# Attention scores and values from stacked high and low halves, with the two row halves of the values summed on VectorE

## The chip, the core and the metric

The kernel runs on one core of a Trainium2 chip. The metric is the device time in microseconds (us) from launch to the end; every time here is of that one core. The engines are TensorE (PE in the profile; its weight loads are PEld), VectorE (DVE), ScalarE (ACT), GpSimd (POOL), and SyncE (SP), which here only issues DMAs.

## The reference

One inference step of a decoder layer for 1024 prompt tokens and 8 sample tokens (T = 1032 rows of 1024 features). The input projection `z = rms_norm(x) @ w_in` gives three convolution inputs, queries (16 heads of 64), keys and values (4 key heads of 64) and two gates. The attention is causal within a window of 128:

```python
def attend(q, k, v, q_pos, k_pos, rel_bias, sinks):
    s = jnp.einsum('...qkgd,...skd->...kgqs', qg, k,
                   preferred_element_type=jnp.float32) * (HEAD_DIM ** -0.5)
...
    s = jnp.where(valid[..., None, None, :, :], s + bias, -jnp.inf)
    m = jnp.maximum(jnp.max(s, axis=-1, keepdims=True), sink)
    p = jnp.exp(s - m)
    p = p / (jnp.sum(p, axis=-1, keepdims=True) + jnp.exp(sink - m))
    o = jnp.einsum('...kgqs,...skd->...qkgd', p.astype(v.dtype), v)
```

The prompt is cut into 8 blocks of 128 queries; a block looks at its own 128 keys and the 128 before. Convolution and attention outputs are projected, gated, added, projected again, and followed by a mixture of 32 experts. All data are float32.

## The kernel before

**Products.** Almost every float32 product is made from two parts: x is rounded to a "high" part (type fp32r, a reduced float32 that TensorE takes) and the rest is the "low" part. The product is the sum of three fp32r matmuls, high*high, high*low and low*high, accumulated in PSUM. ScalarE writes the high part with a copy, VectorE subtracts it from the original to get the low part. Weights come in units of 1024 rows by 128 columns (`w_raw`, three slots), are split to `w_hi` and `w_lo` (`split_hi` L1127, `split_lo` L1433), and are used in three chunks of 344 tokens, 24 matmuls each, into the PSUM banks `DN[0..2]`.

**Stages.** (A) Ten weight units for queries and keys, into `q_sb` and `k_sb`; (V) two units for the values, nine chunks of 24 matmuls, into `v_sb`; (B) the prompt's attention, woven into the 24 units of the convolution inputs; (C) 32 units of output projections and gates; then the output projection with routing, and the experts.

**Stage B** is what the change is about. It runs 8 blocks (`step_b(j)`); block j makes three convolution units and the attention of query block j. A block has nine steps i = 0..8. In step i TensorE does, in this order of its program (L830 to L850):

- `scores(i)` for i < 8 (L796): two heads at once (one in partitions 0 to 63, the other in 64 to 127), each one plain float32 matmul of 64 rows: 128 queries by 256 keys, from `q_stage` and `k_stage`, into PSUM banks `SCB`. It waits for `max_ready` of step i-1;
- the 24 matmuls of convolution chunk i (L847 to L849), k = 0..7. Between them stand `values` (at k = 2 of steps 3, 5, 7 for steps 1, 3, 5, and at k = 5 of the next block's step 0 for step 7) and `turn_probs(i-1)` at k = 5 (L806, four transposes of the probabilities).

`values` (L825 to L827) makes, for each of two key heads and each of two key tiles, three matmuls of 256 columns: `v_hi`*`probsT_hi`, `v_hi`*`probsT_lo`, `v_lo`*`probsT_hi`. The stationary operand holds both key heads of a pair, 128 columns, so that half of the 128 result rows is of use; the other half is thrown away. Twelve matmuls for a full block, six in block 0, which has one key tile.

VectorE in step i, in order: maxima of the scores with the bias (L1543 to L1549, `max_ready`), in step 1 the low part of v (L1555), the inverse of the sums (L1512, L1513; waits for ScalarE's exponentials), the low part of the turned probabilities of step i-1 (L1563; waits for ScalarE's high part, and so for TensorE's transposes), in steps 6 and 7 the convolution itself (L1570 to L1576), `leave(i)`, which takes chunk i out of PSUM (L1524, L1527, L1532; waits for TensorE's chunk i), and in steps 0, 3, 6 one `split_lo` (L1433). ScalarE in step i: exponentials (L1183, L1184), high part of the turned probabilities of step i-1 (L1192), `store_o` (L1165; in step 6 and in the next block's step 1: the attention output from PSUM to `q_sb`), the scaling of the probabilities (L1199, `probs_normed`, for which `turn_probs` waits), and in steps 0, 3, 6 `split_hi`. GpSimd copies the next block's k and q to `k_stage` and `q_stage` (L551, L552) once the eight scores of a block are done.

Engines run their own programs in order and wait on semaphores. The order is written out by hand.

**Weight slots.** SyncE loads a unit into `w_raw[slot]` once the slot's `split_lo` is done (`lo_ready`); `w_lo` is a buffer of its own.

## Time and profile before

| | us |
|---|---|
| three runs | 1740.86, 1736.86, 1737.24 |
| median | 1737.24 |
| profiled execution: its own time | 1738.65 |
| profiled execution: span of the trace | 1737.1 |
| stage B in the trace: first scores to the first chunk of C | 187.8 to 585 |

The profile was taken on one execution; its own time is 1.4 us above the median, and 1.5 us of it lie outside the span of the trace. In rows of the timeline the first number is the start, the second the length; matmuls overlap their neighbours, so the price of one matmul is the distance between two starts and not its length. "x4" means that so many instructions are merged in one row; the plain float32 matmuls leave two records each. A pair in brackets at the end of a row gives the idle time of the engine before it and who ended it.

### The profile page before, as it was taken

Reading aid. Unit: us, or ns where it says so; the run is one execution under the profiler, and the core shown is the slowest. Engines: PE = TensorE matmul, PEld = TensorE weight load, DVE = VectorE, ACT = ScalarE, POOL = GpSimd, SP = SyncE. Lnnn points to the kernel's source line nnn. Section 1 sums busy time; section 2 is a strip of 40 time slices with the busy share of each in tenths; the row PEclk is TensorE's granted clock in tenths of the full one; section 3 lists DMA queues with packets and bytes.
Section 4 is the critical chain, followed back from the end, with each engine's and each line's share of the span. In section 5 each row is a group of like instructions: output and inputs, shape, how many; then the busy total and the mean of one; then the engine's idle time right before and its main releaser. Section 6 shows DMA issues by size and latency. Waiting matters only on the chain. (4 is left out here: it accounts for less than half of the span.)

```text
span 1737.1 us, 26183 instructions
## 1 busy us (share of the span) xinstructions
PE 1653.6 (95%) x9527; PEld 1474.4 (85%) x9527; DVE 1036.5 (60%) x1839; ACT 834.0 (48%) x1202; POOL 234.0 (13%) x197
## 2 busy tenths in 40 slices
PE   5999999999999999999999999699999999999991
PEld 4899899999999999999999888478888888877871
DVE  5322466656556432114222576788989899888883
ACT  5000355555555430113112211378788888877773
POOL 1100000000000100000000111322322323222310
PEclk9999999999999999999999999799999999999996
DMA  6242111111111301114113711799999999999956
GB/s 161 79 125 86 40 41 46 49 36 36 36 49 48 101 25 49 49 36 158 41 44 120 255 73 72 266 379 375 379 375 372 381 370 380 373 368 367 365 206 218
DMA packets 131856, 305.30 MB, mean 176 GB/s; under 512 B 30403, under 2 KB 92079, under 8 KB 106935
## 3 DMA queue, kind: packets, MB, share of 16 engines
q1 hardware_dynamic: 115415, 267.76, 42.2%
q0 software_dynamic: 16384, 36.76, 7.3%
q8 instruction: 38, 0.62, 0.1%
q14 instruction: 19, 0.16, 0.0%
HBM read 282.81 MB, written 40.41 MB: 186 GB/s over the span
## 5 line engine op out<-in xcount | busy, mean ns | idle before, releaser
L1847 DVE TENSOR_TENSOR e_lo<-e_raw,e_hi 128x2048 fp32r<-128x2048 f32 x192 | 434.5, 2287 | 58.6 <-ACT e_hi L1332 34.1
L1332 ACT ACTIVATE e_hi<-e_raw 128x2048 fp32r<-128x2048 f32 x192 | 366.1, 1921 | 64.6 <-PE bank L1033 30.2
L1031 PE MATMUL bank<-e_hi,xT_hi 128*128 128x512 f32 x512 | 206.8, 404 | 6.7 <-DVE xT_lo L1852 6.7
L1127 ACT ACTIVATE w_hi<-w_raw 128x1024 fp32r<-128x1024 f32 x68 | 71.6, 1053 | 284.4 <-PE bank L704 252.8
L702 PE MATMUL bank<-h_hi,w_hi 128*128 128x344 f32 x624 | 202.8, 325 | 1.1 <-DVE h_lo L1452 1.1
L1033 PE MATMUL bank<-e_hi,xT_lo 128*128 128x512 f32 x512 | 202.5, 395 | 0.0
L1032 PE MATMUL bank<-e_lo,xT_hi 128*128 128x512 f32 x512 | 201.9, 394 | 0.0
L703 PE MATMUL bank<-h_lo,w_hi 128*128 128x344 f32 x624 | 199.9, 320 | 0.0
L704 PE MATMUL bank<-h_hi,w_lo 128*128 128x344 f32 x624 | 199.8, 320 | 0.0
L847 PE MATMUL bank<-h_hi,w_hi 128*128 128x344 f32 x576 | 197.3, 342 | 2.0 <-DVE w_lo L1433 2.0
L848 PE MATMUL bank<-h_lo,w_hi 128*128 128x344 f32 x576 | 184.8, 321 | 0.0
L849 PE MATMUL bank<-h_hi,w_lo 128*128 128x344 f32 x576 | 184.4, 320 | 0.0
L1433 DVE TENSOR_TENSOR w_lo<-w_raw,w_hi 128x1024 fp32r<-128x1024 f32 x68 | 84.6, 1245 | 153.5 <-ACT w_hi L1127 152.4
L1183 ACT ACTIVATE probs<-probs,negm 128x256 f32<-128x256 f32 (+1 forms) x128 | 62.4, 488 | 140.1 <-DVE sinkd L1549 140.1
L847 PEld LDWEIGHTS bank<-h_hi,w_hi 128*128 128x128 f32 x576 | 108.8, 189 | 21.6 <-issue 9.9
L1031 PEld LDWEIGHTS bank<-e_hi,xT_hi 128*128 128x128 f32 x512 | 96.6, 189 | 32.1 <-issue 6.7
L702 PEld LDWEIGHTS bank<-h_hi,w_hi 128*128 128x128 f32 x624 | 117.9, 189 | 5.0 <-issue 3.5
L704 PEld LDWEIGHTS bank<-h_hi,w_lo 128*128 128x128 f32 x624 | 118.0, 189 | 0.0
L703 PEld LDWEIGHTS bank<-h_lo,w_hi 128*128 128x128 f32 x624 | 117.8, 189 | 0.0
L1033 PEld LDWEIGHTS bank<-e_hi,xT_lo 128*128 128x128 f32 x512 | 96.7, 189 | 23.1
L1032 PEld LDWEIGHTS bank<-e_lo,xT_hi 128*128 128x128 f32 x512 | 96.7, 189 | 20.5
L848 PEld LDWEIGHTS bank<-h_lo,w_hi 128*128 128x128 f32 x576 | 109.2, 190 | 0.0
(327 smaller groups left out, 3134.6 us busy)
## 6 DMA issues: line engine op xcount, KB each, us to landing
e_raw<-in_w_e_gate_dram SPq DMA_DIRECT2D x64, 1024.0 KB
e_raw<-in_w_e_up_dram SPq DMA_DIRECT2D x64, 1024.0 KB
e_raw<-in_w_e_down_dram SPq DMA_DIRECT2D x64, 1024.0 KB
w_raw<-in_w_in_dram SPq DMA_DIRECT2D x104, 256.0 KB, 3.1
a_spill<-y_sb POOLq DMA_DIRECT2D x8, 516.0 KB, 2.9
a_raw<-a_spill SPq DMA_DIRECT2D x2, 2064.0 KB, 9.6
x_tok<-in_x_prompt_dram SPq DMA_DIRECT2D x4, 1024.0 KB, 10.7
w_raw<-in_w_attn_out_dram SPq DMA_DIRECT2D x32, 128.0 KB, 2.9
```

Source lines behind the costliest of these rows:

```text
L702: pe.matmul(out, wh, xh, start=i == 0, stop=False)
L703: pe.matmul(out, wh, xl, start=False, stop=False)
L704: mm = pe.matmul(out, wl, xh, start=False, stop=i == len(pairs) - 1)
L847: pe.matmul(DN[c][:, 0:CH], w_hi[:, s, k, :], h_hi[:, k, cols], start=k == 0, stop=False)
L848: pe.matmul(DN[c][:, 0:CH], w_hi[:, s, k, :], h_lo[:, k, cols], start=False, stop=False)
L849: mm = pe.matmul(DN[c][:, 0:CH], w_lo[:, s, k, :], h_hi[:, k, cols], start=False, stop=k == KT - 1)
L1031: pe.matmul(out, xT_hi[:, par, kk, :], wh, start=kk == 0, stop=False)
L1032: pe.matmul(out, xT_hi[:, par, kk, :], wl, start=False, stop=False)
L1033: mm = pe.matmul(out, xT_lo[:, par, kk, :], wh, start=False, stop=kk == KT - 1)
L1332: A.activation(e_hi[:, slot % 4, :], e_raw[slot][:, :], ACT.Copy).then_inc(e_hi_done, 1)
L1433: V.tensor_tensor(w_lo[:, slot, :, :], w_raw[slot][:, :, :], w_hi[:, slot, :, :].bitcast(F32), ALU.subtract).then_inc(lo_ready, 1)
L1847: V.tensor_tensor(e_lo[slot][:, :], e_raw[slot][:, :], e_hi[:, slot % 4, :].bitcast(F32), ALU.subtract).then_inc(e_lo_done, 1)
```

## The change

- **Scores.** `q_a` holds, for the even head, the high part of q in partitions 0 to 63 and its low part in 64 to 127; `q_b` the same for the odd head with the halves the other way round. `kk_hi` holds the high part of k twice, in both halves; `kk_lo` the low part twice. One fp32r matmul over all 128 rows gives (q_hi + q_lo) * k_hi; a second (q_hi + q_lo) * k_lo. So four fp32r matmuls of 256 columns stand where two plain float32 ones of 64 rows stood.
- **Values.** `vv` holds for each key head its high and low columns side by side as one 128-column stationary operand. Two matmuls (with `probsT_hi`, with `probsT_lo`) take the place of three; one half of the result rows is from v_hi, the other from v_lo, and both are needed.
- **New work.** GpSimd makes the high parts in their own halves (four copies of 64 partitions per four steps, `stage`); ScalarE makes the two copies of k's high part in the other halves (`twin`); VectorE makes the low parts (`stage_low`, six subtractions of 64 partitions); ScalarE now copies the result half of the low part to `o_rest`, and VectorE adds it to the other half (`add_rest`), which takes over `o_stored`. Each of these is done twice per block, for heads 0 to 7 (t = 0) and 8 to 15 (t = 1).
- **Buffers.** To make room, `w_lo` now lies on top of `w_raw`, slot by slot. A slot is free for the next load only when TensorE has used it (`chunk_done`), and the slots of the units are renumbered.

```diff
-        q_stage = at("q_stage", R5, [KT, P])
-        k_stage = at("k_stage", R5 + 4096, [2, 2 * P])
+        q_a = at("q_a", R5, [KT, P], F32R)
+        q_b = at("q_b", RING + 24576, [KT, P], F32R)
+        kk_hi = at("kk_hi", RING + 28672, [KV, 2 * P], F32R)
+        kk_lo = at("kk_lo", RING + 32768, [KV, 2 * P], F32R)
...
-        w_lo = at("w_lo", RING + 24576, [3, KT, P], F32R)
+        w_lo = at("w_lo", RING, [3, KT, P], F32R)
...
+        twin_done, TWIN_FROM = sqrt_done, 3
+        stage_lo, STAGE_FROM = x_scaled, 9
+        rest_done, REST_FROM = h_hi_done, 16
...
                 if wait is not None:
-                    sp.wait_ge(lo_ready, wait)
+                    sp.wait_ge(chunk_done, wait)
...
+            def stage(b, t):
+
+                if not isinstance(b, int):
+                    pool.wait_ge(scores_ready, b * 8 + (4 * t - 4))
+                st = slice(4 * t, 4 * t + 4)
+                pool.tensor_copy(q_a[0:64, st, :], q_sb[0:64, st, bass.ds(b * P, P)])
+                pool.tensor_copy(q_b[64:128, st, :], q_sb[64:128, st, bass.ds(b * P, P)])
...
+                pool.tensor_copy(kk_hi[0:64, 2 * t, keys], k_sb[0:64, bass.ds(t, 1), old].rearrange("p a s -> p (a s)"))
+                pool.tensor_copy(kk_hi[64:128, 2 * t + 1, keys], k_sb[64:128, bass.ds(t, 1), old].rearrange("p a s -> p (a s)")).then_inc(staged, 1)
...
-                if st == 0:
-                    pe.wait_ge(staged, b * 2 + 2)
+                if st % 4 == 0:
+                    pe.wait_ge(staged, b * 2 + (t + 1))
+                    pe.wait_ge(twin_done, b * 2 + (TWIN_FROM + t + 1))
+                    pe.wait_ge(stage_lo, b * 2 + (STAGE_FROM + t + 1))
...
                 for h in range(2):
-                    mm = pe.matmul(SCB[h][:, place + off:place + 256], q_stage[64 * h:64 * h + 64, st, :],
-                                   k_stage[64 * h:64 * h + 64, t, off:256], start=True, stop=True)
+                    q2, out = (q_a, q_b)[h], SCB[h][:, place + off:place + 256]
+                    pe.matmul(out, q2[:, st, :], kk_hi[:, 2 * t + h, off:256], start=True, stop=False)
+                    mm = pe.matmul(out, q2[:, st, :], kk_lo[:, 2 * t + h, off:256], start=False, stop=True)
...
-                        vh, vl = v_hi[:, kt, P * t:P * t + P], v_lo[:, kt, P * t:P * t + P]
-                        ph, pl = probsT_hi[:, h, kt, :, :], probsT_lo[:, h, kt, :, :]
-                        pe.matmul(out, vh, ph, start=kt == kts[0], stop=False)
-                        pe.matmul(out, vh, pl, start=False, stop=False)
-                        mm = pe.matmul(out, vl, ph, start=False, stop=kt == 1)
+                        v2 = vv[:, kt, t, 2 * h:2 * h + 2, :].rearrange("p a d -> p (a d)")
+                        pe.matmul(out, v2, probsT_hi[:, h, kt, :, :], start=kt == kts[0], stop=False)
+                        mm = pe.matmul(out, v2, probsT_lo[:, h, kt, :, :], start=False, stop=kt == 1)
...
                 for h in range(2):
-                    rows = slice(64 * h, 64 * h + 64)
-                    ins = A.activation(q_sb[rows, 4 * t:4 * t + 4, bass.ds(b * P, P)], OB[h][rows, :].rearrange("p (k t) -> p k t", k=4), ACT.Copy)
-                ins.then_inc(o_stored, 1)
+                    ins = A.activation(o_rest[64 * h:64 * h + 64, :], OB[h][64 - 64 * h:128 - 64 * h, :], ACT.Copy)
+                ins.then_inc(rest_done, 1)
...
+                A.activation(kk_hi[64:128, 2 * t, keys], k_sb[0:64, t, old], ACT.Copy)
+                A.activation(kk_hi[0:64, 2 * t + 1, keys], k_sb[64:128, t, old], ACT.Copy).then_inc(twin_done, 1)
...
+            def stage_low(b, t, first=False):
+
+                dve.wait_ge(staged, b * 2 + (t + 1))
+                dve.wait_ge(twin_done, b * 2 + (TWIN_FROM + t + 1))
...
+                V.tensor_tensor(q_a[64:128, st, :], q_sb[0:64, st, now], q_a[0:64, st, :].bitcast(F32), ALU.subtract)
+                V.tensor_tensor(q_b[0:64, st, :], q_sb[64:128, st, now], q_b[64:128, st, :].bitcast(F32), ALU.subtract)
...
+                    for dst in (own, other):
+                        ins = V.tensor_tensor(kk_lo[dst, 2 * t + h, keys], k_sb[own, t, old], kk_hi[own, 2 * t + h, keys].bitcast(F32), ALU.subtract)
+                ins.then_inc(stage_lo, 1)
+
+            def add_rest(t, b):
+
+                dve.wait_ge(rest_done, b * 2 + (REST_FROM + t + 1))
+                for h in range(2):
+                    rows = slice(64 * h, 64 * h + 64)
+                    ins = V.tensor_tensor(q_sb[rows, 4 * t:4 * t + 4, bass.ds(b * P, P)], o_rest[rows, :].rearrange("p (k t) -> p k t", k=4),
+                                          OB[h][rows, :].rearrange("p (k t) -> p k t", k=4), ALU.add)
+                ins.then_inc(o_stored, 1)
...
                 for i in range(9):
+                    if i == 2 and not first:
+                        stage_low(j, 1)
+                    if i == 5 and not last:
+                        stage_low(j + 1, 0)
...
+                    if i == 1 and not first:
+                        add_rest(1, j - 1)
+                    if i == 6:
+                        add_rest(0, j)
...
+            stage_low(0, 0, True)
+            stage_low(0, 1, True)
```

ScalarE calls `twin(j, 1)` at the start of step 2 and `twin(j + 1, 0)` at the start of step 5, VectorE `stage_low` at the same two places. Before block 0 VectorE has `stage_low(0, 0)` and `stage_low(0, 1)` behind its last work of stage V.

The order on VectorE, from the low part of v in step 1 to the maxima of step 2. Before:

```order
L1555 TENSOR_TENSOR v_lo<-v_sb,v_hi 128x512
L1512 TENSOR_TENSOR rden<-den,esink 128x2
...
L1513 RECIPROCAL rden<-rden 128x2
L1563 TENSOR_TENSOR probsT_lo<-bank,probsT_hi 128x4x128
...
L1524 COPY u_sb<-bank 128x344
...
L1540 MEMSET carrier 128x1
```

and now:

```order
L1530 TENSOR_TENSOR rden<-den,esink 128x2
...
L1612 TENSOR_TENSOR probsT_lo<-bank,probsT_hi 128x4x128
...
L1553 TENSOR_TENSOR q_sb<-o_rest,bank 64x4x128
...
L1566 COPY u_sb<-bank 128x344
...
L1539 TENSOR_TENSOR q_a<-q_sb,q_a 64x512
...
L1540 TENSOR_TENSOR q_b<-q_sb,q_b 64x512
...
L1545 TENSOR_TENSOR kk_lo<-k_sb,kk_hi 64x256 x2
...
L1586 MEMSET carrier 128x1
```

Two additions (L1553 stands twice) now come before `leave(1)`, and six subtractions (L1545 stands twice, two each) between `leave(1)` and the maxima of step 2, which begin with the MEMSET. In front of the maxima of step 5 the same six stand, and in step 6 the two additions behind the low part of the probabilities.

The order on TensorE at a step's start, between the last matmul of one convolution chunk and the first of the next:

```order
L865 MATMUL bank<-h_hi,w_lo 128x344
L814 MATMUL bank<-kk_hi,q_a 128x256
L815 MATMUL bank<-kk_lo,q_a 128x256
L814 MATMUL bank<-kk_hi,q_b 128x256
L815 MATMUL bank<-kk_lo,q_b 128x256
L863 MATMUL bank<-h_hi,w_hi 128x344
```

Before, one row stood there, L796, with its two matmuls of 64 rows; nothing else of TensorE's order at this place moved.

## Rows read from the trace of the kernel before

**Rows 1.** The page's engines; a window of stage B (PE, PEld, DVE, ACT, POOL, clock)
```profile
PE 1653.6 (95%) x9527; PEld 1474.4 (85%) x9527; DVE 1036.5 (60%) x1839; ACT 834.0 (48%) x1202; POOL 234.0 (13%) x197
...
260.00:640.00 380.00, 380.00 (x2550) 348.65 (x2549) 209.58 (x680) 189.27 (x496) 23.22 (x25) 0.99 0.15 48
```

**Rows 2.** Timeline of PE, scores of steps 0, 1, 2 of a block, and the next block
```profile
333.64 0.70 PE L796 MATMUL bank<-k_stage,q_stage 64*128 64x256 f32 x4
339.69 0.70 PE L796 MATMUL bank<-k_stage,q_stage 64*128 64x256 f32 x4
344.72 0.70 PE L796 MATMUL bank<-k_stage,q_stage 64*128 64x256 f32 x4
...
383.59 0.70 PE L796 MATMUL bank<-k_stage,q_stage 64*128 64x256 f32 x4
```

**Rows 3.** Timeline of PE around one pair of scores
```profile
399.50 0.31 PE L849 MATMUL bank<-h_hi,w_lo 128*128 128x344 f32 x1
399.74 0.70 PE L796 MATMUL bank<-k_stage,q_stage 64*128 64x256 f32 x4
400.37 0.42 PE L847 MATMUL bank<-h_hi,w_hi 128*128 128x344 f32 x1
400.63 0.32 PE L848 MATMUL bank<-h_lo,w_hi 128*128 128x344 f32 x1
```

**Rows 4.** The same at the end of a `values`; then line L827 alone
```profile
402.59 0.28 PE L826 MATMUL bank<-probsT_lo,v_hi 128*128 128x256 f32 x1
402.71 0.28 PE L827 MATMUL bank<-probsT_hi,v_lo 128*128 128x256 f32 x1
...
L827 PE MATMUL bank<-probsT_hi,v_lo x120: 277/280/283, 206.8 to 584.7; 128*128 128x256 f32 x120
```

**Rows 5.** Timeline of DVE, steps 3 to 5 of a block
```profile
357.38 1.22 DVE L1433 TENSOR_TENSOR w_lo<-w_raw,w_hi 128x1024 fp32r<-128x1024 f32 x1 [0.51 <-ACT w_hi L1127]
358.53 0.48 DVE L1543 CUSTOM_DVE_ANT_0 probs<-bank,bias_sb,sink 128x256 f32<-128x256 f32 x1
...
362.17 0.50 DVE L1527 TENSOR_TENSOR u_sb<-u_sb,bank 128x344 f32<-128x344 f32 x1
362.60 0.48 DVE L1543 CUSTOM_DVE_ANT_0 probs<-bank,bias_sb,sink 128x256 f32<-128x256 f32 x1
```

**Rows 6.** Timeline of DVE, then of POOL, from step 6 to step 7 of a block
```profile
372.15 0.69 DVE L1563 TENSOR_TENSOR probsT_lo<-bank,probsT_hi 128x512 fp32r<-128x512 f32 x1 [0.56 <-ACT probsT_hi L1192]
...
375.35 0.99 DVE L1574 SCALAR_TENSOR_TENSOR y_sb<-histT,cols,y_sb 128x8 f32<-128x8 f32 x1
...
377.62 0.48 DVE L1543 CUSTOM_DVE_ANT_0 probs<-bank,bias_sb,sink 128x256 f32<-128x256 f32 x1
...
374.29 2.04 POOL L552 COPY q_stage<-q_sb 128x1024 f32 x1
```

**Rows 7.** Timeline of ACT: `store_o` in step 6, scaling of step 7, two blocks
```profile
330.69 0.90 ACT L1199 ACTIVATE probs<-probs,rden 128x256 f32<-128x256 f32 x2
372.01 1.18 ACT L1165 ACTIVATE q_sb<-bank 64x512 f32 x2
380.65 0.90 ACT L1199 ACTIVATE probs<-probs,rden 128x256 f32<-128x256 f32 x2
```

**Rows 8.** Timeline of DVE, steps 0 and 1 of a block
```profile
339.79 0.52 DVE L1524 COPY u_sb<-bank 128x344 f32<-128x344 f32 x1 [2.16 <-PE bank L849]
...
341.37 0.48 DVE L1543 CUSTOM_DVE_ANT_0 probs<-bank,bias_sb,sink 128x256 f32<-128x256 f32 x1
```

**Rows 9.** Groups by line and form: 512 elements in blocks 1 to 7, 256 in block 0
```profile
L1555 DVE TENSOR_TENSOR v_lo<-v_sb,v_hi 128x512 fp32r<-128x512 f32 x7 | 4.8, 693 | 0.5
...
L1563 DVE TENSOR_TENSOR probsT_lo<-bank,probsT_hi 128x256 fp32r<-128x256 f32 x8 | 3.4, 422 | 4.3 <-ACT probsT_hi L1192 4.3
```

**Rows 10.** Timeline of PE at the start of stage B, then a window (clock 0.50)
```profile
187.83 0.49 PE L796 MATMUL bank<-k_stage,q_stage 64*128 64x128 f32 x4
190.36 0.42 PE L847 MATMUL bank<-h_hi,w_hi 128*128 128x344 f32 x1 [2.04 <-DVE w_lo L1433]
...
192.00:194.00 2.00, 2.00 (x8) 2.00 (x8) 0.19 (x2) 1.73 (x6) 0.00 (x0) 0.50 0.79 236
```

**Rows 11.** Timeline of PE, start of stage V
```profile
160.69 0.58 PE L780 MATMUL bank<-w_hi,h_hi 128*128 128x256 f32 x1 [3.13 <-DVE w_lo L1433]
```

More of the change, by code:

```diff
@@ L559, in _ @@
             pool.wait_ge(bias_loaded, 16)
-            stage(0, True)
+            for t in range(2):
+                stage(0, t)
             flat = lambda x: x.rearrange("b s g d -> b s (g d)")
@@ L569, in _ @@
             with pool.Fori(0, KT - 1) as j:
-                stage(j + 1, False)
+                for t in range(2):
+                    stage(j + 1, t)
                 spill(j)
@@ L779, in _ @@
                     xh, xl = h_hi[:, k, P * n:P * n + rows], h_lo[:, k, P * n:P * n + rows]
-                    pe.matmul(out, xh, w_hi[:, 0:2, k, :], start=k == 0, stop=False)
-                    pe.matmul(out, xh, w_lo[:, 0:2, k, :], start=False, stop=False)
-                    mm = pe.matmul(out, xl, w_hi[:, 0:2, k, :], start=False, stop=k == KT - 1)
+                    pe.matmul(out, xh, w_hi[:, 0:3:2, k, :], start=k == 0, stop=False)
+                    pe.matmul(out, xh, w_lo[:, 0:3:2, k, :], start=False, stop=False)
+                    mm = pe.matmul(out, xl, w_hi[:, 0:3:2, k, :], start=False, stop=k == KT - 1)
                 mm.then_inc(chunk_done, 1)
@@ L1120, in _, with split_hi @@
             step = Steps(act, act_step)
-            def split_hi(u, slot, uses, freed):
+            def split_hi(slot, uses):
                 act.wait_ge(raw_loaded[slot], uses * 32)
-                if freed is not None:
-                    act.wait_ge(chunk_done, freed)
                 A.activation(w_hi[:, slot, :, :], w_raw[slot][:, :, :], ACT.Copy).then_inc(hi_ready, 1)
@@ L1143, in _ @@
                 if g == 0:
-                    split_hi(0, 0, 1, None)
-            def splits_a(t):
-                split_hi(t * 5 + 1, 1, t * 2 + 1, None if isinstance(t, int) and t == 0 else t * 15)
-                split_hi(t * 5 + 2, 2, t + 1, t * 15 + 3)
-                split_hi(t * 5 + 3, 0, t * 2 + 2, t * 15 + 6)
-                split_hi(t * 5 + 4, 1, t * 2 + 2, t * 15 + 9)
-                split_hi(t * 5 + 5, 0, t * 2 + 3, t * 15 + 12)
-            splits_a(0)
-            with act.Fori(1, 2) as t:
-                splits_a(t)
-            split_hi(U_V + 1, 1, 5, 30)
-            split_hi(U_B, 0, 6, 39)
+                    split_hi(0, 1)
+            for slot, uses in ((1, 1), (2, 1), (0, 2), (1, 2), (0, 3), (1, 3), (2, 2), (0, 4), (1, 4)):
+                split_hi(slot, uses)
+            split_hi(0, 5)
+            split_hi(2, 3)
+            split_hi(1, 5)
             def store_o(t, b):
@@ L1497, in _ @@
                 units_a(t, False)
-            split_lo(U_V + 1, 1)
+            split_lo(U_V + 1, 2)
             for n in range(NT):
@@ L1534, in step_b @@
                 for i in range(9):
+                    if i == 2 and not first:
+                        stage_low(j, 1)
+                    if i == 5 and not last:
+                        stage_low(j + 1, 0)
                     if i < 8:
@@ L1586, in _ @@
             n1 = step.n
-            with dve.Fori(1, KT) as j:
+            with dve.Fori(1, KT - 1) as j:
                 step.n = j * per + (n1 - per)
                 step_b(j, False)
-            step.n = n1 + (KT - 1) * per
-            split_lo(U_C + 1, 1)
+            step.n = n1 + (KT - 2) * per
+            step_b(KT - 1, False, True)
+            assert step.n == n1 + (KT - 1) * per
+            add_rest(1, KT - 1)
+            split_lo(U_C + 1, 0)
             for i, (dst, src) in enumerate(((k_out[:, 0, :], bank[3][:, 0:256]), (k_out[0:B8, 1, :], bank[4][0:B8, 0:256]),
@@ L1602, in _ @@
             ins.then_inc(q_new_done, 1)
-            split_lo(U_C + 2, 0)
+            split_lo(U_C + 2, 1)
             dve.wait_ge(kcT_psum, 4)
@@ L1634, in _ @@
             ins.then_inc(so_stored, 1)
-            split_lo(U_C + 4, 0)
+            split_lo(U_C + 4, 1)
             for k in range(KT):
@@ L1648, in _ @@
             for n in range(AHEAD, 2 * AHEAD):
-                split_lo(U_C + n + 1, (n + 1) % 2)
+                split_lo(U_C + n + 1, n % 2)
                 projected(n, n - AHEAD)
```

172 lines of the change are left out of this document (93 added, 79 removed).

## The prediction

> **What bounds the kernel now.** I read the page first: PE is busy 95% of the span, DVE 60%, ACT 48%. The window 260 to 640 us, nearly all stage B, has PE busy for all of its 380 us, DVE for 55% and ACT for 50% [rows 1]. A busy share doesn't tell whether PE works at its pace, so I went to the timeline of PE. The scores of step 0 start at 333.64 in one block and at 383.59 in the next: 49.95 us per block, the same in all seven full blocks [rows 2]. A step without `values` takes 5.03 us (339.69 to 344.72); step 0, with a `values`, 6.05. I can account for that from PE's own work: 24 matmuls at 0.157 are 3.77, four transposes some 0.45, the scores some 0.8. So PE bounds stage B, and no wait of PE on another engine is left in it but small change.
>
> The second thing to read is how far behind the others are, since the change moves work from PE to them. VectorE and ScalarE form a chain inside each step: maxima, exponentials, inverse of the sums, low part of the probabilities, `leave`. Where nothing makes that chain wait for PE, one step of it takes 4.07 us (start of the maxima 358.53 to 362.60 [rows 5]). A busy share of 55% hides that: most of VectorE's idle time in that step is its wait for ScalarE's exponentials, and new work of VectorE can't be put there, because its program is in order. So the slack of the chain, not VectorE's idle share, decides.
>
> **What the change takes from PE.** Scores: between the last matmul of a chunk (399.50) and the second of the next (400.63) lie 1.13 us [rows 3]; two matmuls at the chunk's pace of 0.157 would be 0.31, so the scores cost 0.82. The new form is four matmuls of 256 columns, 128 rows, fp32r. That form stands in `values`, at a distance of 0.12 (402.59 to 402.71) [rows 4]: 4 x 0.117 = 0.47. Saved: 0.35 per step, 2.8 per block. Values: four matmuls fewer of twelve, 0.47 each time, four times per block: 1.87. PE would need 49.95 - 2.8 - 1.9 = 45.3 us per block. Over the kernel L827 stands 120 times [rows 4], one third of `values`: 120 x 0.117 = 14.0 us; scores 64 x 0.35 = 22.4 us, if block 0 (128 columns) saves the same. In all 36 us of PE's time.
>
> A rule speaks against the scores' part. The rows show four records of the scores, each some 0.4 long, inside 0.70 us [rows 3]: the two heads run at the same time. The Trainium skill (TensorE: Matmul & The Clock Gate, "Why this matters for your kernels") says that matmuls of few rows in different row groups run concurrently, which the trace bears out. By that rule alone the pair has the price of one matmul and four serial ones cost more; by the rows the pair costs 0.82, as plain float32 takes several passes, and the four cost 0.47. I go by the rows.
>
> **What it puts on VectorE.** `stage_low` has two subtractions of 512 elements per partition and four of 256. The nearest rows are the low part of v, 128x512, 0.693 us, and that of the first block's probabilities, 128x256, 0.422 [rows 9]. One behind the other they overlap by 0.08 (362.17 to 362.60 is 0.43 for an instruction of 0.50 [rows 5]), so 2 x 0.61 + 4 x 0.34 = 2.58 us. That they cover 64 partitions I count as no gain; bounds: 1.3 (half) and 3.6 (no overlap, some contention). `add_rest`: 2 x 0.61 = 1.22, bounds 0.6 and 1.8. Both come twice per block: 7.6 us of work in order. ScalarE: `store_o` keeps its size (1.18 for its two [rows 7]); `twin` adds two copies of 256 elements, some 0.9 us, twice per block; no row shows it, bounds 0.5 and 1.5. GpSimd: 3072 elements per partition instead of 1536 per block; its copy of 1024 took 2.04 us [rows 6], so 3 to 4 us in place of 2.6, hidden, since it has over a step until `stage_low` asks.
>
> **The loop that these lie in.** From the maxima of step 1 to the maxima of step 1 of the next block every link is a dependence or an order, with these lengths today: four steps at 4.07 = 16.3; step 3 with its `split_lo`, 4.07 + 1.15 + the wait of 0.51 for w_hi [rows 5] = 5.7; step 6 to the end of L1563, 4.07 - 0.43 = 3.64; from there (372.76) through the convolution and a `split_lo` to the maxima of step 7 (377.62) 4.86 [rows 6]; maxima 7 to the end of the scaling (381.55, [rows 7]) 3.93; from the end of the same scaling one block earlier (331.59) over PE (`turn_probs(7)`, rest of chunk 8, scores 0, chunk 0, `values`) to `leave(0)` at 339.79 [rows 7, 8] 8.20; `leave(0)` and `split_lo` to the maxima of step 1 (341.37) 1.58 [rows 8]. Sum 44.2, against 49.95 of PE: the loop has 5.7 us of slack.
>
> The change adds 7.6 and two waits: in step 5 VectorE waits for `twin`, which ScalarE starts only behind its scaling of step 4 (I take 0.5, bounds 0 and 0.9), in step 6 for `o_rest`, made behind the high part of the probabilities (1.18 long against the 0.61 of L1563: 0.5). It takes 0.35 + 0.47 from the part on PE. 44.2 + 7.6 + 1.0 - 0.8 = 52.0. GpSimd: today one of VectorE's small instructions, 8 elements, took 0.99 us while GpSimd's copy ran [rows 6], and L1573 also ran long; the copies now are longer and come twice, so I add 0.3. **52.3 us per block against 49.95: VectorE's chain becomes the bound**, and PE waits 7 us per block, where it had none. The Trainium skill (SBUF — State Buffer) says that GpSimd and a VectorE instruction with two SBUF inputs lock each other out of a shared port; the 0.99 agrees. By it the six subtractions would be hit too, if they met the copies; the copies start at scores 3 and 7 and end well before.
>
> PE will be seen to wait at four places: scores 3 for `max_ready` of step 2, which is behind the first `stage_low`; `values(1)` and scores 6 likewise; `values(5)` for `o_stored`, which is now at the end of a chain PE, ScalarE, VectorE in step 6; `turn_probs(7)` for the scaling of step 7.
>
> **The sum**, against the profiled execution's 1738.65:
> - seven blocks x 2.35 = +16.5.
> - Start of stage B: today the first chunk starts 2.53 after the first scores, 2.04 of it a wait for `w_lo` [rows 10]. Now VectorE has `split_lo` and then `stage_low(0,0)` (2 x 0.61 + 4 x 0.2 = 2.0) before the scores, which begin some 4 us later than today, the chunk 1.9 later: +1.9. Block 0 has one `stage_low` and one `add_rest` inside, 3.8 us, in a block with some slack: +1.6 (0 to 3.8).
> - Start of stage V: PE waits 3.13 us for `w_lo` of the second unit [rows 11], whose high part could only be made when TensorE had left the slot. With the new slots it is ready before. -1.0.
> - Clock: after the wait of 2.04 us at the start of stage B the granted clock fell to 0.50, 1.2 GHz, for the window 192 to 194 [rows 10]. The forecast has PE waiting one to two us several times per block; where it falls, PE's time doubles for a while, but mostly under a chain that waits less for PE. +3 (0 to 12).
> - Weight slots: a load is issued one unit (11.3 us) before its use; the pieces I can see (load, `split_hi`, `split_lo` 1.22 [rows 5]) fit in that. 0.
>
> Sum +22.0: 1760.7 on the profiled execution; it stood 1.4 above the median, so in terms of the median 1737.24, **1760 us**, 1.3% slower.
>
> **Rivals.**
> 1. *The additions are hidden, PE stays the bound.* For it: DVE is idle 45% of stage B. Against: that idle time is inside the chain of 4.07 us. It needs the additions to cost under the slack left beside PE's 45.3, that is 45.3 - 43.4 = 1.9 us per block in place of 8.6. Then 36 us go, less 1.9 at the start, plus the 1.0 of stage V: 1702. Chance 0.10.
> 2. *Half hidden*: 64-partition work at the lower bounds (1.3 and 0.6, 3.8 per block), no waits. The loop is 44.2 + 3.8 - 0.8 = 47.2, 2.7 under today, 7 x 2.7 = 19 less, and with the start's +2.5: 1720; up to 1742 between that and the forecast. Chance 0.10, mostly in its upper part.
> 3. *The clock falls in every block and the contention is large*: at 3.6 and 1.8 for the two additions, 44.2 + 10.8 + 1.8 - 0.8 = 56, 6 over today: 42 us, with the start 1782; with upper bounds of one of them alone about 1775. Chance 0.18.
> 4. *The scores are no cheaper* (the four full-height matmuls take plain float32's passes): then PE is at 48 to 50 per block beside the chain of 52; it changes the time little, since the chain bounds. It lies inside the forecast.
>
> The forecast itself has 0.62. What a measurement of this kernel can tell from no change is 0.3%, 5.2 us. Faster 0.12 (rival 1 and the lowest part of 2), same 0.08, slower 0.80. The range 1744 to 1782 leaves out rival 1, the lower part of 2 and the top of 3.
>
> **What would show it.** In the profile after: block period from scores 0 to scores 0 at 52.3 (PE's bound 45.3); distance of the four scores matmuls 0.12; `stage_low` from its first start to the maxima 2.6 us, `add_rest` 1.2; idle of PE before scores 3, `values(5)` and `turn_probs(7)`, with VectorE or ScalarE as releasers; first chunk of B later by 2; wait before V down from 3.1 to 2. I am wrong if the period is under 49, or if PE's waits end on a DMA (the slots).

## The result and the profile after

The changed kernel takes 1779.64 us (median of four runs, 1778.39 to 1785.16), the kernel before 1738.52 beside it: ratio 1.0244, 95% interval 1.0229 to 1.0260. Forecast were 1760 us in a range of 1744 to 1782. The time lies inside the range, 2.4 us below its upper end. The sign and the place were right; the size was 41 us instead of 22.

The page after, to be read beside the one of before [rows 1]: the span, busy time by engine, and the same window of stage B (columns: PE, PEld, DVE, ACT, POOL, granted clock, share and rate of the DMA engines).

```profile
span 1777.5 us, 26176 instructions
PE 1633.7 (92%) x9407; PEld 1475.8 (83%) x9407; DVE 1099.3 (62%) x1967; ACT 847.1 (48%) x1234; POOL 248.3 (14%) x245
...
260.00:640.00 380.00, 329.51 (x2173) 318.65 (x2172) 256.89 (x755) 187.68 (x501) 30.05 (x57) 0.98 0.14 44
```

PE did 20 us less than before (1653.6 then) and the kernel got 41 us longer: in the window PE is busy for 329.5 of 380 us where it had been busy for all of them. The starts of the scores of step 0 (timeline of PE) give the new period:

```profile
456.39 0.28 PE L814 MATMUL bank<-kk_hi,q_a 128*128 128x256 f32 x1
...
510.87 0.28 PE L814 MATMUL bank<-kk_hi,q_a 128*128 128x256 f32 x1
...
565.38 0.28 PE L814 MATMUL bank<-kk_hi,q_a 128*128 128x256 f32 x1
```

54.5 us per block where it was 49.95 [rows 2]. What PE waits for in these two blocks (columns: line, releaser; us in all, times, longest):

```profile
PE bank L814 <- DVE sinkd L1595: 7.2, 4, 2.5
PE bank L842 <- DVE q_sb L1553: 5.1, 2, 2.6
PE bank L842 <- DVE probsT_lo L1612: 1.9, 2, 0.9
PE bank L824 <- ACT probs L1217: 1.8, 2, 0.9
```

These are the places that the forecast names: scores 3 and 6 (L814), `values(5)` for `o_stored` and `values(1)` (L842), `turn_probs(7)` (L824). They make 8.0 us per block. The chain behind scores 3, on DVE: the sum of the halves, chunk 1, `stage_low`, and only then the maxima of step 2.

```profile
467.15 1.38 DVE L1553 TENSOR_TENSOR q_sb<-o_rest,bank 64x512 f32 x2
468.55 0.52 DVE L1566 COPY u_sb<-bank 128x344 f32<-128x344 f32 x1
469.10 0.69 DVE L1539 TENSOR_TENSOR q_a<-q_sb,q_a 64x512 fp32r<-64x512 f32 x1
469.80 0.69 DVE L1540 TENSOR_TENSOR q_b<-q_sb,q_b 64x512 fp32r<-64x512 f32 x1
470.50 1.72 DVE L1545 TENSOR_TENSOR kk_lo<-k_sb,kk_hi 64x256 fp32r<-64x256 f32 x4
...
472.25 0.48 DVE L1589 CUSTOM_DVE_ANT_0 probs<-bank,bias_sb,sink 128x256 f32<-128x256 f32 x1
```

Where the 40.4 us between the two spans arise, by landmarks of PE: up to the first scores +1.7; block 0 -0.7 (45.9 for 46.6); blocks 1 to 6 +30.9 (the start of block 7 less that of block 1 is 329.9 for 299.0); block 7 and the first four units of stage C, up to the first product with `o_hi`, +4.1 (118.7 for 114.6); from there to the end +4.3 (6.9 from the first product with `o_hi` to the last with `a_hi`, and 2.6 less behind that). The last I had not expected at all: nothing of the attention is left there, only the new use of the weight slots. What lies behind `a_hi` took between 768.3 and 774.3 us in the fourteen traces of this case, so that the 2.6 are no effect of the change that could be told from chance.

### The profile page after: what moved, and what is told of

It reads as the page before. It is cut to its first block and busy times, and to the rows that moved or that the text cites. A ratio compares the mean times of both kernels' runs of the same rounds, so it can differ in the third digit from the quotient of the medians.

```text
span 1777.5 us, 26176 instructions
## 1 busy us (share of the span) xinstructions
PE 1633.7 (92%) x9407; PEld 1475.8 (83%) x9407; DVE 1099.3 (62%) x1967; ACT 847.1 (48%) x1234; POOL 248.3 (14%) x245
## 5 line engine op out<-in xcount | busy, mean ns | idle before, releaser
L717 PE MATMUL bank<-h_hi,w_hi 128*128 128x344 f32 x624 | 203.3, 326 | 1.1 <-DVE h_lo L1470 1.1
L863 PE MATMUL bank<-h_hi,w_hi 128*128 128x344 f32 x576 | 192.5, 334 | 0.0
## 6 DMA issues: line engine op xcount, KB each, us to landing
a_raw<-a_spill SPq DMA_DIRECT2D x2, 2064.0 KB, 13.1
```

The source lines that it names most:

```text
L717: pe.matmul(out, wh, xh, start=i == 0, stop=False)
L863: pe.matmul(DN[c][:, 0:CH], w_hi[:, (s + 1) % 3, k, :], h_hi[:, k, cols], start=k == 0, stop=False)
```

## The experiments

Theory A, formed from the two traces: VectorE's program, in its order, sets the period of stage B, and the weight slots cost stage C some 6 to 10 us. Its rivals stand in each expectation. "Period" is the distance of the first scores of two blocks in the run's own trace, in blocks 2 to 6. Each run had runs of the kernel before on its chip; these were 1736.78 in the first set of four, 1738.89 in the second, 1737.37 in the third (three kernels), 1738.08 beside the last.

### The parts by themselves

**Slots alone** (`slots_only`). Scores, values and staging as before:

```diff
-        w_lo = at("w_lo", RING + 24576, [3, KT, P], F32R)
+        w_lo = at("w_lo", RING, [3, KT, P], F32R)
...
-                    sp.wait_ge(lo_ready, wait)
+                    sp.wait_ge(chunk_done, wait)
```

> The kernel before with the change's buffers alone: w_lo on top of w_raw, loads that wait for TensorE's use of a slot, the new slot numbers; scores, values and all staging as before. Theory A (what the two traces say: after the change the stages behind B lose another 10 us, in waits of TensorE for w_hi's followers and in clock drops): B keeps its period of 49.95 us, C becomes 6 to 10 us longer, 1745 to 1749 us. Rival B (my forecast: a load issued one unit ahead fits, slots cost nothing): 1738 to 1740 us. Rival C (late loads also stretch the blocks of B, period over 50.5): 1753 us or more.

1739.44 us, ratio 1.0021 (1.0011 to 1.0031). Period 49.9. The time is rival B's, the mechanism is neither's: the slots give and take. Stage B starts 2.8 us earlier (first scores 185.03 for 187.83), and block 0 is 2.4 shorter: its wait for `w_lo` is 1.21 instead of 2.04 and the granted clock stays at full speed behind it; then C is longer. Products with `o_hi` and with `a_hi` (min/median/max ns, first and last start), before and with the slots alone:

```profile
L702 PE MATMUL bank<-o_hi,w_hi x192: 316/319/428, 648.0 to 784.2; 128*128 128x344 f32 x192
L702 PE MATMUL bank<-a_hi,w_hi x192: 317/320/342, 807.3 to 965.4; 128*128 128x344 f32 x192
```

```profile
L712 PE MATMUL bank<-o_hi,w_hi x192: 317/320/426, 642.8 to 780.9; 128*128 128x344 f32 x192
L712 PE MATMUL bank<-a_hi,w_hi x192: 317/320/427, 804.8 to 965.8; 128*128 128x344 f32 x192
```

In these lines the first product with `a_hi` comes 162.0 us after the first with `o_hi`, where it was 159.3. From the first `o_hi` to the last `a_hi` 323.0 us instead of 317.4. So my 0 for the slots was near the truth in sum, by two errors that cancel: 5.2 us gained ahead of block 1, 5.6 lost in C.

**w_lo in a place of its own in stage C** (`c_own`), where `q_b` and `kk_hi` are no longer needed; stage B as in the change. Loads wait for `split_lo` again, and ScalarE's `split_hi` gets a wait for TensorE's last use of the slot (not shown):

```diff
+        w_lo_c = at("w_lo_c", RING + 24576, [2, KT, P], F32R)
...
             def c_freed(n):
 
-                return 105 if isinstance(n, int) and n == 0 else n * 3 + 108
+                if isinstance(n, int) and n < 2:
+                    return chunk_done, (105, 111)[n]
+                if isinstance(n, int) and n == 2:
+                    return chunk_done, 114
+                return lo_ready, n + (U_C - 1)
```

> The changed kernel, but from the second unit of stage C on w_lo lies in a place of its own (where q_b and kk_hi lay, dead by then), and loads wait for split_lo again. Stage B is untouched. Theory A (C's extra 10 us are the slots'): 1779.6 - 10 = 1770 us, 1767 to 1773. Rival (C's extra waits and clock drops come from something that B leaves behind, such as TensorE's idle time before them): 1776 to 1781 us.

1774.24 us, ratio 1.0208 (1.0195 to 1.0221), 0.36% or 6 us under the changed kernel's ratio. The trace has the stretch from the first `o_hi` (683.3) to the last `a_hi` (1000.8) at 317.5, as before, where the changed kernel has 324.3. Theory A in the mechanism, with 6 of its 10 us; the time itself lies between the two ranges, 1.2 us above theory A's. How it comes about shows in the changed kernel around `a_raw`: ScalarE's copy of a unit waits for a load that could be issued only when TensorE had left the slot (at 833.79, behind the bulky `a_raw` at 823.29 in the same queue), and `a_hi` and `a_lo` stand behind it.

```profile
840.79 1.06 ACT L1141 ACTIVATE w_hi<-w_raw 128x1024 fp32r<-128x1024 f32 x1 [6.68 <-DMA w_raw<-in_w_conv_out_dram]
841.75 3.92 ACT L1292 ACTIVATE a_hi<-a_raw 128x1032 fp32r<-128x1032 f32 x4
...
846.11 0.40 PE L717 MATMUL bank<-a_hi,w_hi 128*128 128x344 f32 x1 [1.18 <-issue]
```

Before, the same copy waited 2.35 us and the first product with `a_hi` did not wait. That the load is late because of `a_raw`, and not only because it is issued late, is argued from this row and not tried.

The same trace shows what the clock costs in stage B. The granted clock fell once in each of these blocks, behind a wait of 2.4 to 2.7 us at scores 3, and yet the blocks took 54.6 us each. PE's own time per block, the period less its waits, rose to 47.6 (46.5 in blocks of the changed kernel at full clock), and the waits fell to 7.0 (8.0). The window of the fall, in columns as before:

```profile
417.00:421.00 4.00, 3.25 (x14) 3.18 (x15) 2.53 (x12) 2.52 (x8) 1.73 (x4) 0.57 0.40 120
```

**Values alone and scores alone** (both with the new slots), the other part as before.

> The change without its scores part: buffers as after, values from stacked halves, o_rest and add_rest; scores plain float32 again, no twin, no stage_low. TensorE's need per block is 49.95 - 4 x 0.47 = 48.1 us, VectorE's loop 44.2 + 2 x 1.40 + 0.4 = 47.4 us. Theory A (TensorE bounds again, C pays 6 to 10 for the slots): 1738.5 - 7 x 1.9 + 8 = 1733 us, 1729 to 1737. Rival (the wait for o_rest and add_rest delays the later steps and so VectorE's chain bounds): period 50 or more, 1746 us or more.

1745.54 us, ratio 1.0045 (1.0031 to 1.0058): the rival in kind, though the period stays 0.1 and the time 0.5 us under its bounds of 50 and 1746. PE's four `values` per block became 0.48 cheaper each (steps of 5.98 instead of 6.46), yet the period stayed at 49.9. The distance from scores 7 to the next block's scores 0 grew from 10.75 to 12.17 and swallowed all of it. PE's waits in 235 to 530 us:

```profile
PE bank L816 <- ACT probs L1198: 7.5, 6, 1.3
PE bank L834 <- DVE q_sb L1516: 1.7, 6, 0.3
```

L816 is `turn_probs(7)`. In step 6 VectorE does `add_rest` behind a wait of 0.65 for `o_rest`, then the convolution, then the maxima of step 7; exponentials and scaling of step 7 are late by that much, and this stretch had little slack. I had counted slack around the whole loop (5.7 us), and there is much less in this stretch. The loss itself lies elsewhere: blocks 1 to 6 took 298.9 us, as with the slots alone (298.8), while block 0 took 1.0 more and the stretch from block 7 to the first `o_hi` 4.8 more. In that stretch PE waits 2.70 us for `q_new`, a copy in VectorE's program behind the blocks, which neither the kernel before nor the slots alone shows.

> The change without its values part: buffers as after, scores from stacked halves with twin and stage_low; values from three products of v_hi and v_lo, store_o by ScalarE alone. TensorE's need per block is 49.95 - 8 x 0.35 = 47.2, VectorE's loop 44.2 + 2 x 3.15 + 1.2 of waits for twin = 51.7. Theory A (VectorE's chain sets the period, stage_low costs its start-to-start time of 3.15 and not the sum of its 2.58): 1738.5 + 7 x 1.8 + 3.5 at the start + 8 in C = 1763 us, 1757 to 1769. Rival (the scores part is what hurts in all, add_rest is covered): 1775 us or more. Rival (stage_low is half hidden): under 1752.

1764.23 us, ratio 1.0156 (1.0143 to 1.0169), period 52.8 to 53.2 instead of the 51.7 worked out. Theory A; the time lies in its range, the period 1.1 to 1.5 above its figure. Values alone +8.8, scores alone +27.5, the slots in both once too often (2.7): 34 us, where the whole is 41. The difference is in blocks 1 to 6: against before, the values part alone adds 0.0 us there, the scores part alone 18.8, both 30.9. So the parts load the same chain, and what one of them still hides alone costs beside the other.

### The price of VectorE's new work

**Without `stage_low` in the loop** (`no_low`) and **without `add_rest`** (`no_rest`), all else as changed.

> The changed kernel without stage_low in the blocks of the loop: the low parts of q and k stay those of block 0 (left out of the computation), everything else of the change is there. This prices VectorE's six subtractions and their waits. Theory A (VectorE's chain sets the period; 2 x 3.15 us of subtractions and 1.2 us of waits for twin go): period from 54.7 to 48 to 49 us, 1779.6 - 7 x 6.2 - 3 = 1733 us, 1727 to 1741. Rival B (the wait of turn_probs(7) behind add_rest, seen with the values part alone, holds the period at 49.9 us): 1779.6 - 7 x 4.8 = 1746 us, 1742 to 1750. Rival C (the subtractions are mostly hidden): over 1755 us.

1737.91 us, ratio 0.9996 (0.9984 to 1.0008), period 48.4:

```profile
428.35 0.28 PE L815 MATMUL bank<-kk_hi,q_a 128*128 128x256 f32 x1
...
476.74 0.28 PE L815 MATMUL bank<-kk_hi,q_a 128*128 128x256 f32 x1
```

Theory A on the period (48 to 49) and in its range, 5 us above its central figure. The six subtractions twice per block, with their waits for `twin`, are worth 6.1 us per block, 43 us in all: as much as the whole loss. What is left are waits of PE for `turn_probs(7)`, 1.3 per block, and before `values(5)` and `values(1)`, 0.7 and 0.5 (rival B's mechanism, at a lower period); in 235 to 525 us:

```profile
PE bank L825 <- ACT probs L1218: 7.6, 6, 1.3
PE bank L843 <- DVE q_sb L1555: 4.1, 6, 0.7
PE bank L843 <- DVE probsT_lo L1610: 3.0, 6, 0.7
```

> The changed kernel without the sum of the two halves: store_o copies the half of the high part from PSUM as before, o_rest and add_rest are left out (so v_lo's product is computed and not used). Theory A (add_rest's 2 x 1.40 and its waits lie on VectorE's chain): period 54.7 to 51.5 to 52.7 us, 1779.6 - 7 x 2.6 = 1761 us, 1756 to 1766; at most the 1764 us of the scores part alone, since TensorE's values are cheaper by 1.9. Rival (the waits before values(5) go, but scores 3 waits instead): 1770 us or more.

1764.16 us, ratio 1.0156 (1.0136 to 1.0176): 15 us for `add_rest`, theory A. Four of the six periods lie between 51.9 and 52.7, the others are 53.9 and 54.4.

**Fewer subtractions** (`half_klo`):

```diff
-                    mm = pe.matmul(out, q2[:, st, :], kk_lo[:, 2 * t + h, off:256], start=False, stop=True)
+                    own = slice(64 * h, 64 * h + 64)
+                    mm = pe.matmul(out, q2[own, st, :], kk_lo[own, 2 * t + h, off:256], start=False, stop=True)
```

> The changed kernel, but the second scores product takes q's high part alone (64 rows), so that k's low part is needed in its own half only: four of the twelve subtractions of a block fall away (2 of 0.43 us each time), nothing else moves. The product of the two low parts is left out. Theory A (VectorE's chain is bare in full): - 2 x 0.86 per block, 1779.6 - 7 x 1.72 = 1767.5 us, 1765 to 1771. Rival (the matmuls over 64 rows lose their cadence of 0.118, or the gap fills with the next wait): 1774 us or more.

1777.91 us, ratio 1.0223 (1.0206 to 1.0240), 2 to 4 us instead of 12. The work on VectorE went, but a step without `values` took PE 5.46 us instead of 4.71. The timeline of PE around one pair of scores:

```profile
357.50 0.32 PE L866 MATMUL bank<-h_hi,w_lo 128*128 128x344 f32 x1
357.66 0.28 PE L814 MATMUL bank<-kk_hi,q_a 128*128 128x256 f32 x1
357.87 0.38 PE L816 MATMUL bank<-kk_lo,q_a 64*128 64x256 f32 x1
358.18 0.38 PE L814 MATMUL bank<-kk_hi,q_b 128*128 128x256 f32 x1
358.49 0.38 PE L816 MATMUL bank<-kk_lo,q_b 64*128 64x256 f32 x1
358.80 0.42 PE L864 MATMUL bank<-h_hi,w_hi 128*128 128x344 f32 x1
359.06 0.31 PE L865 MATMUL bank<-h_lo,w_hi 128*128 128x344 f32 x1
```

With all four at 128 rows they start 0.12 apart, as forecast:

```profile
354.73 0.28 PE L814 MATMUL bank<-kk_hi,q_a 128*128 128x256 f32 x1
354.85 0.28 PE L815 MATMUL bank<-kk_lo,q_a 128*128 128x256 f32 x1
354.97 0.28 PE L814 MATMUL bank<-kk_hi,q_b 128*128 128x256 f32 x1
355.08 0.28 PE L815 MATMUL bank<-kk_lo,q_b 128*128 128x256 f32 x1
```

The rival's first half holds: at each change between 64 and 128 rows the next start is 0.21 to 0.31 away, so a pair costs 1.25 (359.06 - 357.50 - 2 x 0.157) instead of 0.47. PE's waits fell to some 1.5 us per block (8.0 in the changed kernel), and its own time, the period less these waits, rose to 52.3 of the period of 53.8. So PE is the bound in this run, and it doesn't tell what the four subtractions would be worth beside the change's matmuls. The pace also sheds light on the old scores, whose 64-row matmuls stand between 128-row ones in the same way [rows 3]: some of their 0.82 may be the two changes and not the passes of plain float32. How much was not tried.

**The subtractions on GpSimd** (`pool_low`), behind its own copies:

```diff
+                pool.tensor_tensor(q_a[64:128, st, :], q_sb[0:64, st, now], q_a[0:64, st, :].bitcast(F32), ALU.subtract)
...
-                    if i == 2 and not first:
-                        stage_low(j, 1)
-                    if i == 5 and not last:
-                        stage_low(j + 1, 0)
```

> The changed kernel with all subtractions of stage_low on GpSimd behind its own copies; nothing is left out. VectorE's chain loses 2 x 3.15 us and the waits for twin. Theory A: like leaving them out, 1733 to 1746 us. Rival B (GpSimd's subtractions take three times VectorE's and are done after scores 4 or scores 0 want them, or hold VectorE up while they run, as the copy did that stretched a 0.16 us instruction to 0.61): over 1755 us.

1755.28 us, ratio 1.0100 (1.0083 to 1.0117): at the edge of rival B, 9 us above theory A. Periods 50.6 to 53.0 where leaving them out gave 48.4. Groups of 250 to 600 us (columns: shapes, count, busy us and mean ns, idle before), GpSimd's and then VectorE's beside them:

```profile
L577 POOL TENSOR_TENSOR q_a<-q_sb,q_a 64x512 fp32r<-64x512 f32 x12 | 21.8, 1813 | 2.1 <-POOL kk_lo L571 2.1
L578 POOL TENSOR_TENSOR q_b<-q_sb,q_b 64x512 fp32r<-64x512 f32 x12 | 15.5, 1295 | 0.7
...
L1550 DVE TENSOR_TENSOR rden<-den,esink 128x2 f32<-128x2 f32 x53 | 15.9, 299 | 62.1 <-ACT esink L1222 62.1
...
L1627 DVE SCALAR_TENSOR_TENSOR y_sb<-u_sb,cols,y_sb 128x1024 f32<-128x1024 f32 x7 | 12.2, 1743 | 0.9 <-DVE y_sb L1626 0.2
```

GpSimd takes 1.3 to 1.8 us for what VectorE does in 0.69, and it was not late: no wait of PE in stage B ends on it. But VectorE's own instructions grew: 299 ns instead of 167 for the sums, 1743 instead of 1284 for the convolution, where the second figure of each pair is that of the run without the subtractions. One such sum of two elements starts while GpSimd works and ends 0.01 us behind it:

```profile
454.92 1.00 DVE L1550 TENSOR_TENSOR rden<-den,esink 128x2 f32<-128x2 f32 x1 [1.25 <-ACT esink L1222]
...
454.63 1.28 POOL L577 TENSOR_TENSOR q_a<-q_sb,q_a 64x512 fp32r<-64x512 f32 x1 [0.18 <-POOL kk_lo L571]
```

This is the contention that the forecast named, and it was larger. PE's wait for `turn_probs(7)` is 2.8 us per block, where it is 1.3 without the subtractions.

### The same work in another place

VectorE waits for the exponentials in each of eight steps, 1.26 us in seven of them and 0.50 in step 1 (9.3 us per block, and not the 10.1 of the expectation below); one of these waits in the changed kernel:

```profile
485.46 0.16 DVE L1530 TENSOR_TENSOR rden<-den,esink 128x2 f32<-128x2 f32 x1 [1.26 <-ACT esink L1202]
```

The reordered kernel (`gaps`) puts the same instructions there, behind the maxima and ahead of the inverse, and takes nothing away:

```diff
+                    if i == 0 and not first:
+                        stage_low(j, 1, part=(0, 2, 3))
+                    if i == 1 and not first:
+                        stage_low(j, 1, part=(1,))
+                    if i == 2 and not first:
+                        add_rest(1, j - 1)
+                    if i == 4 and not last:
+                        stage_low(j + 1, 0, part=(0, 2))
+                    if i == 5 and not last:
+                        stage_low(j + 1, 0, part=(1, 3))
+                    if i == 6:
+                        add_rest(0, j)
+                    if i == 7 and not last:
+                        stage_low(j + 1, 0, part=(4, 5))
                     if i < 8:
                         invert_sums(i, j)
```

(0 and 1 are the subtractions for `q_a` and `q_b`, 2 to 5 those for `kk_lo`; 4 and 5 of t = 1 stand ahead of `leave(2)`. Besides, ScalarE's `store_o(0, j)` moves to the head of step 6, and VectorE no longer waits for `twin`.)

> The changed kernel with the same instructions in another order; nothing is left out or added. VectorE waits 1.26 us for the exponentials in each of the eight steps of a block, 10.1 us in all; stage_low is cut into pieces and put there (head pairs 0 to 3 of the next block in steps 4, 5 and 7, pairs 4 to 7 in steps 0 and 1, two subtractions left at the start of step 2), add_rest in steps 6 and 2, store_o to the head of ScalarE's step 6, and VectorE no longer waits for twin. Theory A (what costs is where the work stands, not how much it is): period from 54.7 to between 46 and 47.5 us, 1779.6 - 7 x 8 = 1724 us, 1717 to 1737, faster than before. Rival B (VectorE's work as such costs, wherever it stands; exponentials and scaling are then late by as much): 1755 us or more. Rival C (the wait of turn_probs(7) at the end of a block stays, as in the run without stage_low): 1738 to 1748 us.

1722.64 us, ratio 0.9912 (0.9896 to 0.9927): theory A, 57 us under the changed kernel. Period 46.6. Two steps of VectorE:

```profile
442.83 0.17 DVE L1595 TENSOR_SCALAR negm<-maxs 128x2 f32<-128x2 f32 x1
443.26 0.69 DVE L1542 TENSOR_TENSOR q_a<-q_sb,q_a 64x512 fp32r<-64x512 f32 x1
443.96 0.42 DVE L1549 TENSOR_TENSOR kk_lo<-k_sb,kk_hi 64x256 fp32r<-64x256 f32 x1
444.46 0.16 DVE L1530 TENSOR_TENSOR rden<-den,esink 128x2 f32<-128x2 f32 x1
...
446.90 0.17 DVE L1595 TENSOR_SCALAR negm<-maxs 128x2 f32<-128x2 f32 x1
```

The step takes 4.07 us (442.83 to 446.90), the pace that it had before the change [rows 5], with 1.12 us of subtractions inside. PE's waits on the attention fell to 0.97 per block (0.75 before `values(1)`, 0.22 for `turn_probs(7)`), so its own need is 45.7, against the 45.3 forecast.

**Only `stage_low` reordered** (`low_gaps`): `add_rest` and `store_o` back where the change has them.

> The reordered kernel (stage_low in pieces in VectorE's waits), but add_rest and store_o back where the change has them. Theory A: as in the run that leaves stage_low out, the waits of turn_probs(7) and values(5) behind add_rest come back, period 48.4 to 48.9 us instead of 46.6, 1722.6 + 7 x 2.0 = 1737 us, 1733 to 1742. Rival (with stage_low in the waits, add_rest in its old place fits beside TensorE's work): 1722 to 1728 us.

1746.58 us, ratio 1.0054 (1.0040 to 1.0068), period 49.5. Theory A in kind (PE waits 1.3 per block for `turn_probs(7)`, 0.7 for the bank of `values(5)`, 1.4 for low parts of the probabilities), but the cost is 24 us and not 14. Of the reordering's 57 us, 24 are the places of `add_rest` and `store_o` (which of the two was not tried), more than the 15 that `add_rest` is worth beside the unordered `stage_low`: with the longer chain gone, it is the next bound.

**The values part alone, in such places, with the old buffers** (`values_gaps`), and **the reordered kernel with `w_lo` of its own in C** (`gaps_own`).

> The kernel before with the values part alone, buffers untouched (o_rest in 2 KB that are free in stage B), add_rest in VectorE's waits of steps 6 and 2 and store_o at the head of ScalarE's step 6. Scores as before. Theory A (with add_rest in a wait, TensorE bounds and its 4 x 0.47 per block come out): period 48.05 instead of 49.95, 1738.5 - 7.5 x 1.9 = 1724 us, 1721 to 1729. Rival (as with the values part alone, turn_probs(7) waits at the end of a block and the period stays 49.9): 1736 to 1741 us.

1724.28 us, ratio 0.9922 (0.9908 to 0.9935), period 48.4 (48.05 worked out). Theory A: the same values part that cost 0.45% with `add_rest` in its old place and the new slots, of which the slots alone are 0.2%, gains 0.8%.

> The order of the run before this one, and w_lo in a place of its own in stage C. Theory A: the two gains add, some 6 us below that run: 1718 us, 1711 to 1731. Rival (the slots in C cost only where B ended late): no difference to that run within 2 us.

1715.84 us, ratio 0.9878 (0.9863 to 0.9893): 6 to 7 us under the run without it, by the ratios and by the medians. The two gains add. It is the fastest version found, 1.2% under the kernel before, with everything computed that the change computes.

## Why the forecast was right and wrong

- **PE's prices: right.** Four scores matmuls start 0.118 apart (354.73 to 355.08), a step without `values` fell from 5.04 to 4.71, `values` became 0.48 cheaper (0.47). PE's need came out as 45.7 (45.3). So going by the rows was right here, and rival 4 is out. The period before was not quite "the same in all seven full blocks": the trace has six distances, the first is 49.25, the others 49.92 to 49.96.
- **VectorE becomes the bound, PE waits at the named places: right.** Leaving `stage_low` out gave 48.4, leaving `add_rest` out mostly some 52, reordering 46.6.
- **The size of the additions: too small.** "One behind the other they overlap by 0.08" was taken from an instruction followed by another kind. Here the starts of L1539, L1540 and L1545 are 0.70 apart for a length of 0.69, and four of 256 elements take 1.72. `stage_low` lasts 3.15 to the maxima (469.10 to 472.25), not 2.58, and `add_rest` 1.40, not 1.22: +1.5 per block. It was inside the bounds that I gave (3.6 and 1.8), but well above the value that I took; with both at the bounds rival 3 has 56 us per block. So the time lies nearer to rival 3's 1782 us than to the forecast's 1760, by the price of the additions and not by a clock that falls in every block.
- **A link that I missed.** PE's wait at scores 3 delays `turn_probs(2)`, for which VectorE then waits:

```profile
480.01 0.69 DVE L1612 TENSOR_TENSOR probsT_lo<-bank,probsT_hi 128x512 fp32r<-128x512 f32 x1 [0.77 <-ACT probsT_hi L1210]
```

  The forecast had step 3 at its old 5.7 (now 6.6, maxima 476.33 to 482.90): +0.8. The chain was walked once with the old waits, not again with the new ones.
- **Waits and contention: near in sum, by terms that cancel.** `twin` 0.73 (0.5), `o_rest` 0.41 (0.5). VectorE's convolution got faster, since GpSimd's copies no longer meet it (1024 elements of L1573 took 1.57 before, the same line now 1.28), while two small instructions ran 0.34 and 0.60 for 0.16. With these, 52.3 becomes 54.5.
- **Start of B and block 0: too high.** PE's wait before stage V is 1.7 (2 forecast, 3.13 before). The first chunk of B came 0.1 later than before, block 1 starts 1.0 later; the terms up to there made +2.5.
- **Clock: +3 came out, in part by luck.** The granted clock fell three times in blocks 1 to 6, each time behind waits of PE. The six blocks take 329.9 us, 2.9 more than six times 54.5; 2.3 of it is one block (columns as in the first window above):

```profile
399.61:418.00 18.39, 16.09 (x111) 15.77 (x110) 13.02 (x41) 9.57 (x27) 0.92 (x2) 1.00 0.27 86
418.00:426.00 8.00, 7.15 (x32) 6.75 (x31) 3.40 (x14) 3.54 (x11) 1.64 (x4) 0.57 0.00 0
426.00:456.39 30.39, 25.84 (x175) 24.94 (x174) 21.76 (x62) 14.99 (x40) 2.06 (x4) 1.00 0.06 17
```

  PE had waited 2.30 and 0.85 us just before (scores 3, `values(1)`); its matmuls then stood 0.29 apart instead of 0.157. Where the clock was down for half as long, the blocks took 0.3 to 0.5 more, and in `c_own`, with one such fall in each block, 0.1. How often and for how long it falls is not the same in each execution: the run of 1785.16 us had a mean granted clock of 0.970, the other three 0.976 to 0.978.
- **Slots: 0 was wrong in both directions**, 5 us gained ahead of block 1 and 5.6 (slots alone) to 6.9 (changed kernel) lost between the first `o_hi` and the last `a_hi`; that 0 was near the sum was luck. I looked at whether a load fits in a unit's time, not at the places where other loads (`a_raw`, 13.1 us to landing) stand in the same queue.
- **"New work of VectorE can't be put there, because its program is in order" was wrong as a reason.** Being in order decides where the work must stand in the program. Put ahead of the instruction that waits, it is hidden. Rival 1 (hidden, 1702 us) was a matter of the order that the change chose, and the reordered kernels come within 21 and 14 us of it.

In sum, 18.4 us between forecast and the profiled execution (+22.0 and +40.4): -1.5 up to block 1; +13.8 in blocks 1 to 6 (30.9 less 6 x 2.35 and the 3 of the clock), of which the two additions are 9 and the missed link 5; +1.7 in block 7 and the units behind it; +4.3 in stage C and later, the slots' 6.9 less 2.6 behind `a_hi` that may be chance. In the units behind block 7 the forecast had no term at all, and PE waits there for VectorE's copy `q_new`, with the clock down behind it (in the kernel before it does not wait there):

```profile
629.77 0.29 PE L908 MATMUL bank<-k_sb,q_new 64*32 64x8 f32 x8 [2.73 <-DVE q_new L1659]
```

## What to carry to other kernels

When an engine gets more work beside a tuned loop, list its waits inside the loop with their lengths, and put the new instructions directly ahead of the one that waits; a table of busy shares shows neither the place nor the price, and the same 9 us of work per block made 57 us of difference by its place. Take the price of repeated instructions from the distance of starts of the same kind and shape. Slack around a loop is not slack in each stretch of it: walk the chain again with the new waits in place, to the end of the block above all.

## What the hardware showed that I had not expected

- A matmul of 64 rows between matmuls of 128 rows costs at each change: starts 0.21 to 0.31 us apart instead of 0.118 (256 columns, fp32r), 0.75 us per step in all. Whether the change of height or the weight load of the short matmul takes the time was not separated.
- VectorE's instructions on 64 partitions, written to the other 64, last as long as those on 128 (0.69 for 512 elements, 0.42 for 256) and start 0.70 and 0.43 apart: no overlap, no gain from half the partitions.
- GpSimd's subtraction of 64x512 takes 1.3 to 1.8 us, and while it runs VectorE's instructions stretch (1284 to 1743 ns for 1024 elements with two SBUF inputs). The Trainium skill (SBUF — State Buffer, "SBUF: two separate sides") says that a GpSimd instruction that reads SBUF and a VectorE instruction with two SBUF inputs lock each other out of a shared pair of ports for a whole instruction; the trace agrees, with the two-element sum that took 1.00 us and ended with GpSimd's subtraction (454.92 + 1.00 against 454.63 + 1.28).
- Behind waits of PE of 2.30 and 0.85 us, 2.6 apart, the granted clock fell from the upper of its two levels (2.4 GHz) to the lower (1.2 GHz): its mean from 418 to 426 us is 0.57. Other blocks with nearly the same waits kept 1.00. What decides it is open.
